# Layer 2's input projections as seven block products instead of eight

## The reference, cut to what matters

```python
hx = rms_norm(x, norm_w[li]) * (1.0 + scale[:, None]) + shift[:, None]
hc = rms_norm(ctx, norm_w[li]) * (1.0 + scale_c) + shift_c
...
def branch_inputs(h):                       # layer 1: w_in is 1024 x 4096
    q, k, v, g = jnp.split(h @ w_in, 4, axis=-1)
    q = rms_norm(q.reshape(bsz, length, C_HEADS, 2, HEAD_DIM), q_norm)
    k = rms_norm(k.reshape(bsz, length, C_HEADS, 2, HEAD_DIM), k_norm)
    v = v.reshape(bsz, length, C_HEADS, C_VDIM)
...
q = apply_rope(q, cos, sin)
k_all = jnp.concatenate([ck, apply_rope(k, cos, sin)], axis=1)
# per head: softmax(q0 k0) - lam * softmax(q1 k1), times v; then a norm per head,
# silu(g) as a gate, @ w_out, gate, and the residual x
```

## Time and profile before

| what | value |
|---|---|
| median of 3 runs (lowest to highest) | 1128.14 us (1127.74 to 1128.78) |
| span of the profiled execution, first to last instruction | 1124.2 us |
| the profiled execution's own time | not shown beyond its span |
| TensorE busy | 1094.7 us, 97% |
| VectorE busy | 587.8 us, 52% |
| ScalarE busy | 356.2 us, 32% |
| share of TensorE in the chain that ended last | 91% |
| that of line 792 alone | 47% |
| mean granted TensorE clock | 0.995 |

### The profile page before, as it was taken

The page is one execution under the profiler, slowest core; times in us unless marked ns, Lnnn a source line. Parts: engine busy times, 40 slices in busy tenths (PEclk is TensorE's granted clock), DMA queues, the critical chain, the costliest instruction groups (busy, mean ns, idle before and its releaser), DMA issues.

```text
span 1124.2 us, 11877 instructions
## 1 busy us (share of the span) xinstructions
PE 1094.7 (97%) x4252; PEld 590.2 (52%) x4252; DVE 587.8 (52%) x1231; ACT 356.2 (32%) x826; POOL 176.5 (16%) x168
## 2 busy tenths in 40 slices
PE   5899999999999999999999999999999999999998
PEld 2665656565554444555544444444555555556654
DVE  0356677597727366776411235501456553458673
ACT  1522212145322344544300121102334334335450
POOL 0201000397623100000000004300012210000000
PEclk9899999999999999999999999999999999999999
DMA  9913440587760110010011041202022030200001
GB/s 354 345 12 77 153 159 6 180 270 246 256 233 23 57 57 1 1 57 1 1 62 70 0 164 39 87 24 75 1 75 75 1 113 1 75 0 1 1 1 75
DMA packets 49822, 96.34 MB, mean 86 GB/s; under 512 B 4260, under 2 KB 6181, under 8 KB 49765
## 3 DMA queue, kind: packets, MB, share of 16 engines
q1 hardware_dynamic: 43845, 84.57, 21.9%
q10 hardware_dynamic: 5664, 10.84, 2.6%
q0 software_dynamic: 256, 0.18, 0.4%
HBM read 91.28 MB, written 4.30 MB: 85 GB/s over the span
## 4 chain that ended last, share of the span: by engine, by line
PE 91%; DVE 3%; DMA 2%; issue 1%; ACT 1%; POOL 1%; ACTq 1%; DVEq 0%; POOLq 0%
PE ps L792 47%; PE ps L1052 11%; PE ps L980 7%; PE ps L1090 4%; PE ps L1112 4%; PE ps L952 2%; PE ps L834 2%; PE ps L1102 2%; PE ps L999 2%; PE ps L1031 2%; PE ps L1021 2%; PE ps L809 2%; PE ps L964 2%; PE ps L884 1%; DMA ring<-in_mod_w_dram 1%
## 5 line engine op out<-in xcount | busy, mean ns | idle before, releaser
L792 PE MATMUL ps<-ring,hT 128*128 128x512 f32 x736 | 321.2, 593 | 2.2 <-ACT y_all L1867 1.2
L792 PEld LDWEIGHTS ps<-ring,hT 128*128 128x128 f32 x736 | 137.6, 190 | 165.6 <-issue 164.5
L792 PE MATMUL ps<-hT,ring 128*128 128x512 f32 (+1 forms) x512 | 169.8, 486 | 1.2 <-ACT pool_mem L1711 0.7
L1912 POOL TENSOR_SCALAR stat<-stat 128x8 f32<-128x8 f32 (+3 forms) x52 | 20.1, 386 | 740.3 <-DVE stat L1441 237.8
L792 PEld LDWEIGHTS ps<-hT,ring 128*128 128x128 f32 x512 | 95.7, 190 | 65.7 <-issue 59.7
L980 PE MATMUL ps<-ring,hT 128*128 128x512 f32 x192 | 88.5, 594 | 0.5 <-ACT pool_mem L1769 0.5
L1052 PE MATMUL ps<-ring,hT 128*128 128x512 f32 x192 | 85.8, 592 | 0.0
L1913 POOL TENSOR_TENSOR stat<-stat 128x8 f32<-128x8 f32 (+3 forms) x52 | 66.9, 1287 | 4.3
L1473 DVE TENSOR_REDUCE stat<-ps 128x1 f32<-128x768 f32 x64 | 60.9, 951 | 10.2 <-PE ps L1090 10.0
L1259 DVE SCALAR_TENSOR_TENSOR pool_mem<-ps,halftap,pool_mem 128x254 f32<-128x254 f32 (+3 forms) x96 | 59.1, 616 | 3.4
L1876 ACT ACTIVATE xs_all<-ps,stat 128x768 f32<-128x768 f32 x64 | 57.3, 903 | 4.0 <-DVE stat L1474 3.5
(11 more groups left out here) (202 smaller groups left out, 1413.4 us busy)
## 6 DMA issues: line engine op xcount, KB each, us to landing
ring<-in_mod_w_dram SPq DMA_DIRECT2D x10, 2048.0 KB, 8.9
ring<-in_od_w_in_dram SPq DMA_DIRECT2D x8, 2048.0 KB, 8.1
ring<-in_ev_w_in_dram SPq DMA_DIRECT2D x7, 2048.0 KB, 9.6
pool_mem<-la_rows_dram SPq DMA_DIRECT2D x24, 512.0 KB, 7.5
ring<-in_ev_w_out_dram SPq DMA_DIRECT2D x4, 1536.0 KB, 6.6
ring<-in_od_w_out_dram SPq DMA_DIRECT2D x2, 2048.0 KB, 8.0
ring<-in_mod_w_dram ACTq DMA_DIRECT2D x1, 2048.0 KB, 9.2
xs_all<-in_x_dram SPq DMA_DIRECT2D x4, 512.0 KB, 12.9
```

The lines of the kernel that those rows point to most:

```text
L792: mm = pe.matmul(bank[:, 0:width], lhs_of(k), rhs_of(k), start=(k == 0), stop=(k == count - 1))
```

## The change

For 19 pairs of token tile pair and slab the 16 blocks of 128 x 512 become seven products of 4 blocks of 128 x 256 each. The left matrix of a pair (256 tokens by 1024) and the slab (1024 by 512) are cut in four quarters each; the seven products are those of Strassen's algebra in Winograd's form. Tiles 4 and 5 of `k1` half 0 stay as they were.

- `sa`: per pair four sums of quarters of `hT`, 512 elements wide, 12 in all, on VectorE, at the start of layer 1. Three go into `xs_all` (and one into `pool_mem`), the fourth in place.
- `tw`: per slab four sums of quarters, 1024 elements wide, 32 in all, on VectorE. The first is made in place in the slab, the others in a third of `ring`, which layer 1's slabs then leave free: they use two places.
- `pr`: the products. Products 0, 2, 4, 6 add up in one bank, 1 and 3 in the other, 5 uses that one too. ScalarE copies 0, 1, 2 to SBUF and 6 to its rows; VectorE adds 3, 4, 5 to such a copy into the rows.
- `post`: square, or tanh and gating, now read the rows in SBUF.
- `pv1` gets a part of bank 7, and `ptr1` waits for the eviction of the product with v before it.
- `x1` is stored to HBM during the last norms (4 DMAs of 512 KB) and loaded again behind the last product (4 DMAs), ahead of the load of the second output slab in SyncE's list.
- `STEP_PRODUCTS` says how many products an attention step takes; at most one rope is put in a step where two don't wait.

```diff
+STEP_PRODUCTS = [4, 4, 3, 4, 3, 4, 6, 4, 4, 6, 4, 4, 6, 4, 4, 6, 3, 1, 3, 3]
+def slab_products(s):
+    kind, n = IN_SLABS[s]
+    out = []
+    for p in SLAB_PAIRS[(kind, n)]:
+        last = p == SLAB_PAIRS[(kind, n)][-1]
+        for i in range(7):
+            piece = [("pr", kind, n, p, i)]
+            if last and s + 1 < len(IN_SLABS) and i % 2 == 0:
+                piece.append(("tw", s + 1, i // 2))
+            if kind != "v1" and i >= 5:
+                piece.append(("post", kind, n, PAIRS[p][i - 5]))
+            out.append(piece)
+    return out
...
 def stages_layer1():
+    st = [("k1", 0, 4), ("norm", 1, NX - 1), ("k1", 0, 5)] + [("tw", 0, j) for j in range(4)]
+    st += [("trn", 1, k, 0) for k in range(KD)]
+    st += [("sa", 0, 0), ("sa", 0, 1), ("rope", "k1", 0, 4), ("sa", 0, 2), ("sa", 0, 3), ("rope", "k1", 0, 5)]
+    st += [("sa", 1, j) for j in range(4)]
+    turns = {10: ("hk", 0, 1), 13: ("hk", 0, 0), 17: ("hq", 0)}
+    ropes = []
+    for s in range(3):
+        for j, piece in enumerate(slab_products(s)):
+            if ropes and piece[-1][0] == "post" and len(ropes) >= 2:
+                st.append(ropes.pop(0))
+            st += piece
+            if ropes and j % 3 == 2:
+                st.append(ropes.pop(0))
+            ropes += [("rope",) + u[1:] for u in piece if u[0] == "post" and u[1] != "g1"]
+            if s == 1 and j in (0, 2, 4, 6):
+                st.append(("sa", 2, j // 2))
+            if s == 2 and j in turns:
+                st.append(turns[j])
...
+        now = [fill.pop(0) for _ in range(STEP_PRODUCTS[n])] if n < len(STEP_PRODUCTS) else [outs.pop(0)]
+        turned = 1
+        for j, piece in enumerate(now):
+            heads = [("rope",) + u[1:] for u in piece if u[0] == "post" and u[1] != "g1"]
+            while heads and len(ropes) >= 2:
+                st.append(ropes.pop(0))
+                turned -= 1
+            st += piece
+            if j == 0:
+                st.append(("comb1", h, t))
+            elif ropes and turned > 0:
+                st.append(ropes.pop(0))
+                turned -= 1
+            ropes += heads
...
+ODD_SLABS = ("k1", "q1", "v1", "g1", "out1")
-    _p = _free_at.index(min(_free_at))
+    _p = min((p for p in range(RING) if p != SUM_PLACE or _k[0] not in ODD_SLABS), key=lambda p: _free_at[p])
+    if _k == ("out0", 1, 0):
+        SUM_PLACE = _p
...
```

SyncE, TensorE, VectorE and ScalarE:

```diff
+                if stage[:2] == ("norm", 1) and stage[2] < NX:
+                    sp.wait_ge(x1_ready, at("out0", 1, stage[2]))
+                    sp.dma_start(x1_dram[stage[2]], x1[:, stage[2], :]).then_inc(x1_spilled, 16)
+                if stage == ("pr", "g1", 1, 1, 6):
+                    sp.wait_ge(unit_ready, UNIT[stage] + 1)
+                    sp.wait_ge(x1_spilled, 16 * NX)
+                    for t in range(NX):
+                        sp.dma_start(x1[:, t, :], x1_dram[t]).then_inc(x1_back[t], 16)
                 for n in FREED.get(UNIT.get(stage), []):
...
+                    if i in (1, 2, 3, 4):
+                        pe.wait_ge(sa_ready, SA[("sa", p, i - 1)] + 1)
+                    if i in (1, 2, 4, 6):
+                        pe.wait_ge(tw_ready, 4 * s + {1: 1, 2: 2, 4: 3, 6: 4}[i])
+                    bank = begin(stage)
+                    for k in range(KSPLIT):
+                        mm = pe.matmul(bank[:, 0:NSPLIT], left[:, k, :], right[:, k, :], start=(k == 0 and i in (0, 1, 5)),
+                                       stop=(k == KSPLIT - 1), skip_group_check=True)
...
+                        wait_done(pe, PV1S[n - 1])
...
+                    if i in (3, 4, 5):
+                        t, half = ((PAIRS[p][0], 1), (PAIRS[p][1], 1), (PAIRS[p][0], 0))[i - 3]
+                        wait_unit(dve, stage)
+                        wait_done(dve, stage[:4] + (5 - i,))
+                        V.tensor_tensor(odd_rows(sub, n, t)[:, half * NSPLIT:(half + 1) * NSPLIT],
+                                        bank_of(stage)[:, 0:NSPLIT], part_sum[5 - i], ALU.add
+                                        ).then_inc(done_sem(stage), 1)
...
+                    if j == 0:
+                        n = SLAB_NO[IN_SLABS[s]]
+                        dve.wait_ge(slab_in[PLACE[n]], LANDED[n])
+                        if s == 0:
+                            wait_unit(dve, ("k1", 0, 5))
+                        last = V.tensor_tensor(b12, b12, b11, ALU.subtract)
+                    else:
+                        if s >= 1:
+                            wait_unit(dve, ("pr",) + IN_SLABS[s - 1] + (SLAB_PAIRS[IN_SLABS[s - 1]][-1], 2 * j))
...
+                    if i in (0, 1, 2, 6):
+                        wait_unit(act, stage)
+                        if i == 6:
+                            dst = odd_rows(sub, n, PAIRS[p][1])[:, 0:NSPLIT]
+                        else:
+                            dst = part_sum[i]
+                            if (sub, n, p) in PAIR_BEFORE:
+                                wait_done(act, ("pr",) + PAIR_BEFORE[(sub, n, p)] + (5 - i,))
+                        if stage == ("pr", "k1", 0, 0, 0):
+                            act.wait_ge(pads_ready, 2)
+                        A.copy(dst, bank_of(stage)[:, 0:NSPLIT]).then_inc(done_sem(stage), 1)
```

More of the change, by code:

```diff
@@ L231, in stages_layer0 @@
     return st
-def stages_layer1():
[L235 to L248, removed]
+PAIRS = ((0, 1), (2, 3), (4, 5))
@@ new lines, in stages_layer1 @@
+def stages_layer1():
+    st = [("k1", 0, 4), ("norm", 1, NX - 1), ("k1", 0, 5)] + [("tw", 0, j) for j in range(4)]
[16 more added lines that the diff above has]
+                st.append(turns[j])
+    assert not ropes
+    fill = [piece for s in range(3, len(IN_SLABS)) for piece in slab_products(s)]
+    outs = [[("out1a", n, t)] for n in range(2) for t in range(NX)]
+    outs += [[("out1b", n, t)] for n in range(2) for t in range(NX)]
@@ L249, in stages_layer1 @@
     work = [(h, t) for h in range(C_HEADS) for t in range(NX)]
     out_turn = {11: 0, 13: 1, 15: 2, 19: 3, 23: 4, 27: 5, 31: 6}
-    ropes = []
-    st.append(fill.pop(0))
+    for _ in range(4):
+        st += fill.pop(0)
     for n in range(len(work)):
@@ L264, in stages_layer1 @@
             st.append(("gates", 1))
[L265 to L268, removed]
+        now = [fill.pop(0) for _ in range(STEP_PRODUCTS[n])] if n < len(STEP_PRODUCTS) else [outs.pop(0)]
[12 more added lines that the diff above has]
+            ropes += heads
+        if ropes and turned > 0 and len(now) < 3:
+            st.append(ropes.pop(0))
         if n >= 1:
@@ L275, in stages_layer1 @@
             st.append(("hnorm", n // 4 - 1))
-    st += [("ptr1",) + work[-1], fill.pop(0), ("pv1",) + work[-1], ("hnorm", C_HEADS - 1)] + fill
+    assert not fill and not ropes
+    st += [("ptr1",) + work[-1]] + outs.pop(0) + [("pv1",) + work[-1], ("hnorm", C_HEADS - 1)]
+    st += [u for piece in outs for u in piece]
     st.append(("otr", C_HEADS - 1))
@@ L313, in unit_banks @@
     bank, turn = [None] * len(UNITS), [None] * len(UNITS)
-    last, turns, held = [-2, -1, -3], [0, 0, 0], set()
+    last, turns, held, sums, cross = [-2, -1, -3], [0, 0, 0], set(), None, None
     for n, s in enumerate(STAGES):
@@ L319, in unit_banks @@
         m = UNIT[u]
+        if u[0] == "pr":
+            i = u[-1]
+            if i in (2, 4, 6):
+                bank[m] = sums
+            elif i == 3:
+                bank[m] = cross
+            else:
+                bank[m] = min((b for b in range(2) if b not in held), key=lambda b: last[b])
+            if i == 0:
+                sums = bank[m]
+                held.add(sums)
+            elif i == 1:
+                cross = bank[m]
+                held.add(cross)
+            elif i == 3:
+                held.remove(cross)
+            elif i == 6:
+                held.remove(sums)
+            turn[m] = turns[bank[m]]
+            turns[bank[m]] += 1
+            last[bank[m]] = n
+            continue
         if bank[m] is None:
-            if m in THREE_BANKS and u[0] != "kvdt":
+            if u[0] == "pv1":
+                bank[m] = 2
+            elif m in THREE_BANKS and u[0] != "kvdt":
                 bank[m] = {"xbc": 1 - u[-1]}.get(u[0], 2)
@@ L932, in _ @@
                     else:
-                        pe.wait_ge(unit_done[2], UNIT_BANK.count(2))
+                        pe.wait_ge(unit_done[2], sum(UNIT_BANK[m] == 2 for m in THREE_BANKS))
                     pe.matmul(ps[:, 7, 0:P], bct[:, 1 - d, c * P:(c + 1) * P], bct[:, 3 - d, c * P:(c + 1) * P],
@@ L1070, in _ @@
                     h, s = a
-                    pe.wait_ge(qk_ready, NT + HEADN[("k1", h // 4, NT - 1)] + 1)
-                    turn(stage, [k1v[:, h // 4, t, h % 4 * P:(h % 4 + 1) * P]
-                                 for t in (range(NX) if s == 0 else range(NX, NT))])
+                    tiles = range(NX) if s == 0 else range(NX, NT)
+                    pe.wait_ge(qk_ready, NT + max(HEADN[("k1", h // 4, t)] for t in tiles) + 1)
```

(1 more changed line is left out.)

159 lines of the change are left out of this document (126 added, 33 removed).

## The result

The changed kernel takes 1143.90 us (median of 4 runs, 1140.69 to 1146.32) against 1127.94 us of the kernel before on the same chip: ratio 1.0148, 95% interval 1.0123 to 1.0172. Run again as it stands it took 1142.99 us, ratio 1.0132 (1.011 to 1.0153). So it is slower by about 16 us, where the forecast said 6: sign and range hold, the size does not.

A forecast was written before the change was run, and what follows sets the result against it. TensorE was taken to bound the kernel. Opening +6.2, attention saving -20.6, attention waits +8, output slab +10 and clock +2 gave +5.6 us on 1128.1: 1133.7, given as 1134, range 1127 to 1141; about 2 in 10 outside 1119 to 1149.

The forecast's parts named there:

- TensorE saves: Over 19 pairs, seven products of 1.72 us replace two units of 6.87: 12.0 us less in the opening, 20.6 in attention.
- hT late (a): From the last tile's transposes to the first product: slab 0's weight sums precede the transposes' evictions on VectorE, +3.9 us.
- opening's stands (b): Layer 1's opening: TensorE waits for VectorE's adds behind ropes and sums, 7.7 us in the first pair, 14.4 in all.
- attention's stands (c): Attention steps 0 to 19: common steps cost nothing, steps with overlong VectorE lists cost 8 us (between 0 and 24).
- second output slab (d): Behind the last product: the slab loads late, after x1's reload, and a scaling waits for it, +10 us (bounds 4 and 15).
- clock: One fall of TensorE's clock to half speed, behind the long wait of step 19: +2 us (bounds 0 and 3).
- Rival E: Products save nothing on TensorE, as weight loads hardly hide; a block takes 0.45 us instead of 0.43: 1145 us, 5%.
- The ropes in the opening: In layer 1's opening, VectorE's adds stand behind ropes of 4.0 us (the first 6.3), so products wait for their bank.
- Transfers: In the opening, x1's four stores and slabs in two places instead of three cost nothing; without cover, stores at most 4 us.
- Rival C: The clock falls at each of the three TensorE waits of 4 us or more: 1138 us, 13%.
- Rival B: Kernel ends faster: adds get their turn within the next product nearly everywhere, 22.4 us of waits shrink to a third: 1119, 22%.
- Rival D: Every attention step loses 1.2 us since ScalarE too waits in order, 24 us instead of 8: 1150 us, 15%.

The follow-up runs named there:

- filled stands: Changed kernel with useless identity matmuls (18, 16, 17 and 36) put into four of TensorE's stands (waits): 1138.22 us, ratio 1.0099 to the kernel before.
- early sums: Changed kernel with slab 0's four weight sums moved before the context tiles' units, the first in its own buffer: 1137.91 us, ratio 1.0094 to the kernel before.
- full: No run: an estimate of the changed kernel's stages with nothing waiting, 94.8 us for the opening, 216.6 for attention steps 0 to 19, 111.1 for the rest.
- late scaling: Changed kernel with the second output slab's eight gate scalings moved from steps 19 to 22 to steps 21 to 23: 1133.03 us, ratio 1.0051 to the kernel before.
- attention reordered: Changed kernel with only attention's order changed (ropes spread over steps 5 to 13, turns moved): 1139.93 us, ratio 1.0108 to the kernel before.
- all reordered: Changed kernel with the opening and attention stages reordered and the second output slab's scaling moved later: 1108.20 us, ratio 0.9824 to the kernel before.

## Why the prediction was off

Each term beside what the stages and runs give (the clock's part taken out by the run with filled stands):

| term | forecast | measured |
|---|---|---|
| TensorE saves | -32.6 | -11.4 - 19.6 = -31.0 |
| hT late (a) | +3.9 | 8.9 - 4.7 = +4.2 |
| opening's stands (b) | +14.4 | 111.3 - 94.8 = +16.5 |
| attention's stands (c) | +8 | 229.8 - 216.6 = +13.2 |
| second output slab (d) | +10 | 119.9 - 111.1 = +8.8 |
| clock | +2 | +6.5 in profiles, 4.8 in medians |

These six come to +18.2, less 0.5 us that before's last stage itself is over 111.1: 17.7, the four stages' sum in the profile. The medians differ by 15 to 16 us; the profiled execution was the slowest of its four. The run with filled stands still has two falls in the opening, so its +16.5 is not stands alone: with early sums the opening has one fall, worth some 1.7 us in its records, and lies 15.2 over full, which leaves an estimated 13.5 for the stands, and the clock costs the more.

- **The seven products.** Right: 1.73 us each in the full opening (94.8 less 3.1, over 53) against 1.72. Rival E (0.45 us a block, 1.80 a product) is out.
- **hT late, slab 0's sums.** Right, 4.2 for 3.9; moving the sums took this away, and with it the low clock on the transposes.
- **The ropes in the opening.** Right in mechanism and nearly in size: product 5 of the first pair was to wait 4.4 us (686.0 to 690.4), and waited 3.7; product 0 of the next slab was to wait 2.6 us twice, and waited 2.5 and 2.0.
- **The second output slab.** Right: its loads end 13.6 us after the reload's issue (1020.9 to 1034.5), as worked out; late scaling took it all away.
- **Transfers.** x1's stores and the two places cost nothing that any stand shows.
- **Attention, the failed step:** "So a common step costs nothing" and the sum of 8 us for single steps. I compared the steps of after with before's minus its units plus 1.73 a product. Step 10 was right in its stand (3.89 for 4.1). Step 10 lost 5.5 us, 1.4 of it by the clock. But the steps with an output turn (11, 13, 15) lost 1.7, 0.9 and 2.0 us, and common steps up to 0.35, 2.8 us together; step 18 lost 1.5, of the 2.2 that were put in for steps 17 to 19. I had followed only adds and ropes. The output's turn is evicted by VectorE and takes the one bank that no pair holds; the next product waits until its eviction has passed the maxima (L1800, 1.79 us twice in the stands). Moving the turns took 3.1 us of that away. Where the 0.3 us of common steps go I did not test. The timeline points at the same bank: in steps 1 and 2 the first product starts 0.15 us after ScalarE's copy of the next head's turn ends (802.91 after 802.77, 814.24 after 814.09), and step 3, which has no turn, loses nothing.
- **The clock, the second failed step:** "I put one such fall, behind the long stand of step 19, into the sum: +2". There were five. Rival C, that it falls at each stand of 4 us, had the right idea, but a stand of 3.7 us did it too, and one of 2.5 us (at 715). That no stretch of layer 1 stood long enough to tell was no evidence for or against it. The Trainium skill, TensorE: Matmul & The Clock Gate (Part 1: The HAM clock gate), says the gate halves the clock after idleness; the trace of after agrees, with 0.50 behind each of its four stands of 3.7 to 8.3 us; two other profiles hold a stand of 3.72 us without a fall (last section). The 4 us that this rule would have added were about the 4.5 us missing here.
- **Rival B** (faster, 22%) named the right lever, the order of adds and ropes, but for a kernel that was not this one: with it reordered the kernel takes 1104 us. Rival D's 1.2 us a step was at most 0.35 in common steps.

So the terms are short by 5.2 us in attention, 4.5 in the clock, 2.1 in the opening's stands (the two falls left in them explain as much), 1.6 in the saving and 0.3 at hT, with 1.2 too much for the slab.

## What to carry to other kernels

Work taken off the bounding engine comes back only if the engine that gets the new work is free at the right moment: here it was 57% busy, and nearly the same operations gave 1144 or 1104 us by their order, with one more buffer. When following such an order by hand, list everything that takes the scarce buffer, not only what the change adds; and put a wait on a late load behind the work that does not need it. Count the granted clock with every stand of several microseconds on TensorE, for what follows may run at half speed.

## What the runs showed of the hardware

The clock does not answer to the length of a stand alone. The stand of 3.72 us before product 5 of the first pair lowered it in the changed kernel (first line), and left it at 1.00 with attention reordered (second line), where the opening's list is the same, and with early sums. The 24 records behind it took 7.97 us in the one and 5.42 in the other:

```profile
694.39 7.97 PE L1205 MATMUL ps<-ring,hT 128*128 128x256 f32 x24 [3.72 <-DVE pool_mem L1713]
```

```profile
691.93 5.42 PE L1210 MATMUL ps<-ring,hT 128*128 128x256 f32 x24 [3.72 <-DVE pool_mem L1718]
```

In the same way the 2.70 us stand in step 12 left it at 1.00 in the run with only attention reordered, and took it to 0.54 in the run with all reordered, where step 12 took 19.8 us instead of 18.1. Windows of the two:

```profile
935.00:937.00 2.00, 2.00 (x11) 1.75 (x10) 1.50 (x5) 0.37 (x1) 1.59 (x1) 1.00 0.00 0
```

```profile
916.00:918.00 2.00, 2.00 (x7) 1.61 (x6) 1.35 (x2) 0.37 (x1) 1.01 (x1) 0.54 0.00 0
```

A fall costs less where TensorE would wait anyway. From the granted clock in windows of 2 us I estimate what the low clock withheld, waits included: 7.1 us of full speed in the opening of the changed kernel and 3.4 with filled stands, yet the stage was only 1.3 us shorter. Behind the stand of step 21 it withheld 2.9 us, and there the stage was 2.4 us shorter. And a matmul of the 128 x 128 float32 identity by itself costs 0.223 us in two records, so filler must be counted from a row of the trace.
